# Rotary embedding in a transformer kernel: permuted operands from SBUF-to-SBUF transfers in place of permutation matmuls

## The chip, the cores and the metric

The kernel runs on one core of a Trainium2 chip. The metric is the device time of one execution in microseconds. TensorE does the matmuls, VectorE (DVE) and ScalarE (ACT) the elementwise work, GpSimd (POOL) and SyncE (SP) here issue transfers for the most part.

## The reference, cut to what matters

Three layers over 256 tokens of width 1024, batch 1, float32: an "even" mixer (stick-breaking attention and top-64 sparse attention with an index score), an "odd" mixer (differential attention), each with a gated feed-forward layer, and a third layer with a chunked recurrence over 272 positions. Queries and keys of the sparse, the index and the differential attention are turned by their position first:

```python
def apply_rope(t, cos, sin):
    t32 = t.astype(F32)
    half = t.shape[-1] // 2
    t1, t2 = t32[..., :half], t32[..., half:]
    return jnp.concatenate([t1 * cos - t2 * sin, t2 * cos + t1 * sin], axis=-1).astype(t.dtype)
...
    o_dsa = dsa_attention(apply_rope(q_dsa.reshape(b, s, N_DSA_HEADS, HEAD_DIM), cos, sin),
                          apply_rope(k_dsa[:, :, None], cos, sin)[:, :, 0],
                          v_dsa,
                          apply_rope(q_ix.reshape(b, s, N_IDX_HEADS, IDX_DIM), cos, sin),
                          apply_rope(k_ix[:, :, None], cos, sin)[:, :, 0],
                          w_ix * N_IDX_HEADS ** -0.5)
...
    q = apply_rope(q.reshape(b, s, 2 * N_DIFF_HEADS, DIFF_DIM), cos, sin).reshape(b, s, N_DIFF_HEADS, 2, DIFF_DIM)
    k = apply_rope(k.reshape(b, s, 2 * N_DIFF_HEADS, DIFF_DIM), cos, sin).reshape(b, s, N_DIFF_HEADS, 2, DIFF_DIM)
```

A head has 64 features, so a half is 32.

## The kernel before, in words

**Layout.** Features lie on partitions, tokens along the free dimension. A tile `qkv[:, n, :]` holds 128 features, two heads, of 256 tokens. The weights come as units of 128x1024 floats (512 KB), two in a 1 MB load by SyncE into `raw`. ScalarE makes `whi` of a unit (L488), VectorE the rest `wlo` (L907), and TensorE computes an output tile of a unit as 8 x 3 matmuls of 128x256 (L1764 to L1766). There are four buffers of `whi` and `wlo` (`SPLIT = 4`): the split of unit m waits until unit m - 4 is done, and both engines work three units ahead (`LEAD = 3`).

**Order.** Each engine runs its instructions in program order. The segments (even, out0, ffn0, down0, odd, out1, ...) follow each other. Within the even segment (20 units) and the odd one (24 units) the attention is written out by hand as pieces ahead of units: TensorE does `even_pieces(u)` or `diff_pieces(u)`, then unit u. VectorE does `even_first(u)` or `diff_first(u)`, then the split of unit u + 3, then `even_then(u)` or `diff_then(u)`; ScalarE likewise. In the odd segment units 0 to 2 run interleaved (`first_units`).

**Rotary embedding.** `trig` holds cosine and sine by partition and token. TensorE multiplies a tile by a constant permutation `rot`, which swaps the halves of each head and negates one, into PSUM (`rotate_even`, L1894, and `rotate`, L2119 and L2120). Keys with one head (tiles 19 and 16) are also needed on both halves of the partitions: `double_even` multiplies them by `dup` and `rotdup` (L1898, L1899). VectorE then computes tile x cos (L1132, L1368), the permuted one x sin (L1133, L1369) and their sum back into `qkv` (L1135, L1371), and counts `rope_done`. The even segment has five such steps, which this text calls rope 0 (tiles 17 and 18), rope 1 (tile 19, doubled), rope 2 (16, doubled), rope 3 (12, 13) and rope 4 (14, 15). TensorE's share stands ahead of units 4, 4, 6, 7 and 9, VectorE's in `even_first` of the same units. The odd segment has eight, rope h for tiles h and 8 + h, which are units 2h and 2h + 1: TensorE's share ahead of unit 2h + 3, VectorE's (`rope_pair`) in `diff_first(2h + 4)`.

**Who needs them.** `index_products` on TensorE ahead of unit 6 (L1913) waits for two `rope_done`; `sparse_scores`, ahead of unit 14, for five. `diff_scores(h)`, L2131, ahead of unit 2h + 6, waits for rope h and for the mask of head h - 1 (`diff_mask`, L1383, VectorE, `diff_first(2h + 5)`), whose exponentials ScalarE computes after unit 2h + 7 (L679), and whose scaling VectorE does in `diff_then(2h + 8)`.

**GpSimd.** Its queue carries the side stream: 40 loads of 1 MB of modulation weights into two buffers (`load_sides`, L2388). Load n waits until 2n - 2 side sums of VectorE are done (`side_used`). The first side sums are those after units 1, 2 and 3; the fourth is at unit 15 (`SIDE_AT`). Loads 36 to 39 wait until the odd segment's attention is done (`o_done`).

## Time and profile before

| | |
|---|---|
| median of 3 runs | 1252.2 us (1250.85 to 1258.83) |
| the profiled execution | 1251.66 us |
| its span, first to last instruction | 1249.9 us |
| mean granted TensorE clock | 0.99 |
| DMA traffic | 232.89 MB, mean 186 GB/s |
| 1 MB weight loads, median to landing | 4.9 us, 177 of them |
| 1 MB side loads, median to landing | 6.9 us, 40 of them |

The page lists busy time by engine, the span in slices, the DMA queues, the chain of work that ended last, and the costliest groups of instructions. A busy TensorE is not a TensorE at its peak, since matmuls are pipelined: their spacing says what one costs. Start times in a timeline are us from the span's start.

### The profile page before, as it was taken

To read this page: it belongs to the slowest core of one execution; us is meant where nothing else is said; L and a number is where in the kernel's file an instruction comes from. 1 tells how busy PE (TensorE), PEld (TensorE's weight loads), DVE (VectorE), ACT (ScalarE), POOL (GpSimd) and SP (SyncE) were. 2 spreads that over 40 slices of the span, in tenths; PEclk is the share of its full clock that TensorE was granted. 3 is DMA by queue.
4 is the path that set the end of the run, shared out by engine and by line. 5 is a ranking of instruction groups with operands and counts; after the bars stand their busy time and mean duration, and the time that the engine had idled before them with its cause. 6 is when DMAs were issued, how large, how long until landed. Compare 5 with 4: busy or idle time off the path is not lost.

```text
span 1249.9 us, 24570 instructions
## 1 busy us (share of the span) xinstructions
PE 1204.4 (96%) x9578; PEld 1171.2 (94%) x9578; DVE 882.8 (71%) x1448; ACT 604.8 (48%) x958; POOL 23.5 (2%) x47
## 2 busy tenths in 40 slices
PE   6999989999998999899999989999999999999997
PEld 6998889999998999899999979998999999999997
DVE  6798778888777785677664467866855685877743
ACT  1558535444344466454443456543433645555532
POOL 0000000000000000000000000000000000000000
PEclk9999989999999999999999999998989999999999
DMA  9944747978782333356455514532322363555541
GB/s 363 357 158 171 277 155 298 353 292 321 257 316 84 135 136 120 151 186 251 169 180 192 179 58 159 179 103 100 136 102 102 137 205 131 202 179 190 176 161 34
DMA packets 35364, 232.89 MB, mean 186 GB/s; under 512 B 4688, under 2 KB 7120, under 8 KB 7504
## 3 DMA queue, kind: packets, MB, share of 16 engines
q1 hardware_dynamic: 29520, 189.78, 42.4%
q0 software_dynamic: 5760, 41.95, 9.3%
q8 instruction: 58, 0.95, 0.3%
q14 instruction: 26, 0.21, 0.0%
HBM read 230.67 MB, written 1.05 MB: 185 GB/s over the span
## 4 chain that ended last, share of the span: by engine, by line
PE 85%; DVE 7%; ACT 4%; issue 3%; DMA 1%; SPq 0%; DVEq 0%; ACTq 0%
PE acc L1764 22%; PE acc L1765 21%; PE acc L1766 21%; PE aux L1764 2%; PE aux L1766 2%; PE aux L1765 2%; PE aux L2256 2%; PE aux L1871 2%; PE aux L1846 2%; ACT whi L488 1%; PE aux L1864 1%; DMA raw<-weights 1%; DVE wlo L907 1%; DVE qkv L1074 1%; PE aux L2131 0%
## 5 line engine op out<-in xcount | busy, mean ns | idle before, releaser
L1764 PE MATMUL acc<-hhi,whi 128*128 128x256 f32 (+3 forms) x1984 | 570.0, 287 | 5.5 <-DVE wlo L907 2.2
L907 DVE TENSOR_TENSOR wlo<-raw,whi 128x1024 fp32r<-128x1024 f32 x338 | 412.5, 1221 | 219.0 <-ACT whi L488 218.9
L1765 PE MATMUL acc<-hlo,whi 128*128 128x256 f32 (+3 forms) x1984 | 562.7, 284 | 0.0
L1766 PE MATMUL acc<-hhi,wlo 128*128 128x256 f32 (+3 forms) x1984 | 560.3, 282 | 0.0
L488 ACT ACTIVATE whi<-raw 128x1024 fp32r<-128x1024 f32 x338 | 356.5, 1056 | 203.1 <-PE acc L1766 186.0
L1764 PEld LDWEIGHTS acc<-hhi,whi 128*128 128x128 f32 x1984 | 376.0, 190 | 10.8 <-issue 6.8
L1766 PEld LDWEIGHTS acc<-hhi,wlo 128*128 128x128 f32 x1984 | 377.4, 190 | 0.0
L1765 PEld LDWEIGHTS acc<-hlo,whi 128*128 128x128 f32 x1984 | 376.3, 190 | 0.4
L1764 PE MATMUL aux<-ahi,whi 128*128 (+1 forms) x264 | 74.3, 281 | 0.0
L1766 PE MATMUL aux<-ahi,wlo 128*128 (+1 forms) x264 | 74.2, 281 | 0.0
L1765 PE MATMUL aux<-alo,whi 128*128 (+1 forms) x264 | 74.1, 281 | 0.0
L1764 PE MATMUL acc<-ahi,whi 128*128 (+1 forms) x264 | 74.1, 281 | 0.0
L1766 PE MATMUL acc<-ahi,wlo 128*128 (+1 forms) x264 | 74.1, 281 | 0.0
L1765 PE MATMUL acc<-alo,whi 128*128 (+1 forms) x264 | 73.9, 280 | 0.0
L1764 PE MATMUL acc<-mhi,whi 128*128 128x256 f32 (+1 forms) x192 | 56.6, 295 | 3.8 <-DVE mlo L926 3.8
L658 ACT ACTIVATE side_conv<-acc 128x256 f32<-128x256 f32 x44 | 16.9, 383 | 79.0 <-PE acc L1766 79.0
L1765 PE MATMUL acc<-mlo,whi 128*128 128x256 f32 (+1 forms) x192 | 54.7, 285 | 0.0
L1766 PE MATMUL acc<-mhi,wlo 128*128 128x256 f32 (+1 forms) x192 | 54.6, 284 | 0.0
L1765 PEld LDWEIGHTS acc<-alo,whi 128*128 128x128 f32 x264 | 49.8, 189 | 0.0
L1765 PEld LDWEIGHTS aux<-alo,whi 128*128 128x128 f32 x264 | 49.8, 189 | 0.0
L1766 PEld LDWEIGHTS aux<-ahi,wlo 128*128 128x128 f32 x264 | 49.8, 188 | 0.0
L1766 PEld LDWEIGHTS acc<-ahi,wlo 128*128 128x128 f32 x264 | 49.7, 188 | 0.0
(346 smaller groups left out, 1503.8 us busy)
## 6 DMA issues: line engine op xcount, KB each, us to landing
raw<-weights SPq DMA_DIRECT2D x177, 1024.0 KB, 4.9
lev<-side_weights POOLq DMA_DIRECT2D x40, 1024.0 KB, 6.9
x<-xT SPq DMA_DIRECT2D x1, 1024.0 KB, 8.9
out<-x SPq DMA_DIRECT2D x4, 256.0 KB, 2.2
cst<-consts SPq DMA_DIRECT2D x1, 768.0 KB, 18.2
cst<-consts SPq DMA_DIRECT2D x1, 584.0 KB, 7.8
cst<-consts SPq DMA_DIRECT2D x1, 256.0 KB, 9.5
vec<-vecs SPq DMA_DIRECT2D x1, 163.0 KB, 2.3
```

Source lines behind the costliest of these rows:

```text
L488: A(whi[:, m % SPLIT, :], raw[:, (m + MOD_UNITS) % RAW, :], ACT.Copy).then_inc(hi_ready, 1)
L658: A(side[:, k % 2, 0:t], acc[(a0 + j) % 4][:, 0:t], ACT.Silu)\
L907: v.tensor_tensor(wlo[:, m % SPLIT, :], raw[:, (m + MOD_UNITS) % RAW, :], whi[:, m % SPLIT, :].bitcast(F32), ALU.subtract).then_inc(lo_rea ...
L1074: ins = v.scalar_tensor_tensor(total, raw[:, u % RAW, :], small[:, u % KT:u % KT + 1], total, ALU.mult, ALU.add)
L1764: mm(o, whi[:, u % SPLIT, w], hi, start=start, stop=False, skip_group_check=True)
L1765: mm(o, whi[:, u % SPLIT, w], lo, start=False, stop=False, skip_group_check=True)
L1766: return mm(o, wlo[:, u % SPLIT, w], hi, start=False, stop=stop_, skip_group_check=True)
L1846: ins = mm(aux[3][:, q:q + 1], mod_sums[s_][:, P * k:P * k + P], C("ones", 1), start=True, stop=True)
L1864: ins = mm(aux[0][:, 0:t], C("mean"), view[:, n, :], start=n == 0, stop=n == KT - 1)
L1871: ins = mm(aux[1][:, 0:t], C("mean"), big[:, 0, n * t:n * t + t], start=n == 0, stop=n == KT - 1)
L2256: ins = mm(o[:, a_:a_ + 64].rearrange("p (n b) -> p n b", b=b), M_[:, h, t0:t0 + P], M_[:, h, t0:t0 + P].rearrange("p (n b) -> p n b", b=2 ...
```

## The change

The products with `rot`, `dup` and `rotdup` are removed from TensorE, with their constants. In their place GpSimd issues transfers from `qkv` to a buffer in SBUF: for a pair of tiles four of 32 partitions x 2 x 256 floats (64 KB), which swap the halves of each head; for a doubled key six, two of 64 partitions x 256 floats (64 KB) and four of 32 partitions (32 KB). There are 24 in the even segment and 32 in the odd one. The sign of the permutation goes into the sine, by a scale per partition. The buffers alternate (`side_conv` in the even segment, `big` in the odd one); VectorE waits for the transfers (`rot_loaded0`, `rot_loaded1`), and GpSimd for VectorE before a buffer is written again. The even transfers stand between side loads 2 and 3 on GpSimd's queue, the odd ones between loads 35 and 36.

```diff
@@ constants
-    ("inv", 1), ("ones", P), ("ident", P), ("rot", P), ("dup", P), ("rotdup", P), ("mean", P), ("mean_v", P),
+    ("inv", 1), ("sign", 1), ("ones", P), ("ident", P), ("mean", P), ("mean_v", P),
...
+    put("sign", np.where(i % 64 < 32, -1.0, 1.0)[:, None])
...
+EVEN_TURNED = (64, 96, 160, 160, 224)
+ODD_TURNED = (224, 160)
...
+        def even_turned(n):
+            return beside_flat[:, 512 * (n % 2):512 * (n % 2) + 512]
+
+        def odd_turned(h):
+            return big[:, 2, 512 + 512 * (h % 2):1024 + 512 * (h % 2)]
@@ ScalarE
-            A(trig[:, 1, :], tile[:, 3, 0:T1], ACT.Sin).then_inc(trig_ready, 1)
+            A(trig[:, 1, :], tile[:, 3, 0:T1], ACT.Sin, scale=C("sign", 1)).then_inc(trig_ready, 1)
@@ VectorE, even_rope
-                dve.wait_ge(rope_mm, n + 1)
+                dve.wait_ge([rot_loaded0, rot_loaded1][n % 2], EVEN_TURNED[n])
...
-                    src, rot = aux[1][:, 0:256], aux[1][:, 256:512]
+                    src, b = b[:, 0:256], b[:, 256:512]
...
-                st(v.tensor_tensor(b, rot, sin, ALU.mult))
+                st(v.tensor_tensor(b, b, sin, ALU.mult))
@@ VectorE, rope_pair
-                dve.wait_ge(rope_mm, 5 + h + 1)
+                dve.wait_ge([rot_loaded0, rot_loaded1][h % 2], ODD_TURNED[h % 2] + 64 * (h // 2 + 1))
@@ TensorE, even_pieces
-                if u == 4:
-                    rotate_even(aux[0], (17, 18), 3)
-                    double_even(19)
...
                 if u == 6:
-                    pe.wait_ge(rope_done, 2)
-                    double_even(16)
                     pe.wait_ge(vt_read, 2)
                     index_products()
-                if u == 7:
-                    pe.wait_ge(relu_done, 4)
-                    rotate_even(aux[0], (12, 13), 6)
-                if u == 9:
-                    pe.wait_ge(rope_done, 4)
-                    rotate_even(aux[0], (14, 15), 8)
@@ TensorE, diff_pieces
-                if 3 <= u <= 17 and u % 2 == 1:
-                    rotate((u - 3) // 2)
@@ GpSimd
-            load_sides(2, 36)
+
+            def turn(b, source, to, of, sem_):
+                pool.dma_start(b[to:to + 32], source[of:of + 32]).then_inc(sem_, 16)
+
+            def turn_even(n, tiles, doubled):
+
+                if n >= 2:
+                    pool.wait_ge(rope_done, n - 1)
+                sem_ = [rot_loaded0, rot_loaded1][n % 2]
+                if doubled:
+                    source, b = qkv[:, tiles, 0:T1], even_turned(n)
+                    for p0 in (0, 64):
+                        pool.dma_start(b[p0:p0 + 64, 0:256], source[0:64]).then_inc(sem_, 16)
+                        turn(b[:, 256:512], source, p0, 32, sem_)
+                        turn(b[:, 256:512], source, p0 + 32, 0, sem_)
+                else:
+                    source = qkv[:, tiles:tiles + 2, 0:T1]
+                    b = even_turned(n).rearrange("p (k t) -> p k t", k=2)
+                    for p0 in (0, 64):
+                        turn(b, source, p0, p0 + 32, sem_)
+                        turn(b, source, p0 + 32, p0, sem_)
+
+            def turn_odd(h):
+
+                for a in range(a0d + 2 * h, a0d + 2 * h + 2):
+                    acc_read(pool, None, a)
+                if h >= 2:
+                    pool.wait_ge(rope_done, 5 + h - 1)
...
+            load_sides(2, 3)
+            pool.wait_ge(even_read, 3)
+            turn_even(0, 17, False)
+            turn_even(1, 19, True)
+            pool.wait_ge(even_read, 4)
+            turn_even(2, 16, True)
+            pool.wait_ge(even_read, 6)
+            turn_even(3, 12, False)
+            pool.wait_ge(even_read, 8)
+            turn_even(4, 14, False)
+            load_sides(3, 36)
+            a0d = START["odd"][2]
+            for h in range(HEADS):
+                turn_odd(h)
```

On TensorE, at the sixth unit of the even segment: before, after unit 5 (`acc<-hhi,whi` and its kin are a unit's matmuls, L1913 the index products).

```order
165 L1766 MATMUL acc<-hhi,wlo 128x256
166 L1898 MATMUL aux<-qkv,cst 128x256 [waits rope_done]
167 L1899 MATMUL aux<-qkv,cst 128x256
168 L1913 MATMUL acc<-qkv 128x128 [waits rope_done,vt_read]
169 L1913 MATMUL acc<-qkv 128x128
170 L1913 MATMUL aux<-qkv 128x128 x2
171 L1913 MATMUL aux<-qkv 128x256 x4
172 L1764 MATMUL acc<-hhi,whi 128x256 [waits even_read,lo_ready]
```

The changed kernel at the same place (its index products are L1901):

```order
161 L1765 MATMUL acc<-hhi,wlo 128x256
162 L1901 MATMUL acc<-qkv 128x128 [waits rope_done,vt_read]
163 L1901 MATMUL acc<-qkv 128x128
164 L1901 MATMUL aux<-qkv 128x128 x2
165 L1901 MATMUL aux<-qkv 128x256 x4
166 L1763 MATMUL acc<-hhi,whi 128x256 [waits even_read,lo_ready]
```

The doubled product of tile 16 is gone, and the index products follow unit 5 directly; they still wait for two ropes.

GpSimd's queue from its first load, before:

```order
6 L2388 DMA lev<-side_weights 128x2048 [waits first_used]
7 L2388 DMA lev<-side_weights 128x2048
8 L2388 DMA lev<-side_weights 128x2048 [waits side_used] x34
9 L2388 DMA lev<-side_weights 128x2048 [waits side_used,o_done]
10 L2388 DMA lev<-side_weights 128x2048 [waits side_used] x3
```

and in the changed kernel, up to the transfers of rope 2:

```order
7 L2354 DMA lev<-side_weights 128x2048
8 L2354 DMA lev<-side_weights 128x2048 [waits side_used]
9 L2367 DMA side_conv<-qkv 32x2x256 [waits even_read]
10 L2367 DMA side_conv<-qkv 32x2x256 x3
11 L2377 DMA side_conv<-qkv 64x256
12 L2367 DMA side_conv<-qkv 32x256 x2
13 L2377 DMA side_conv<-qkv 64x256
14 L2367 DMA side_conv<-qkv 32x256 x2
15 L2377 DMA side_conv<-qkv 64x256 [waits rope_done,even_read]
16 L2367 DMA side_conv<-qkv 32x256 x2
```

The ten transfers of ropes 0 and 1 stand behind the third side load and its wait.

VectorE between its third side sum and the splits of units 7 and 8, before:

```order
56 L937 SCALAR_TENSOR_TENSOR big<-lev,small,big 128x1024 [waits side_used,side_loaded1]
57 L1132 TENSOR_TENSOR lev<-qkv,trig 128x512 [waits rope_mm]
58 L1133 TENSOR_TENSOR lev<-aux,trig 128x512
59 L1135 TENSOR_TENSOR qkv<-lev 128x2x256 [waits dve_step]
60 L1132 TENSOR_TENSOR lev<-aux,trig 128x256 [waits rope_done,rope_mm]
61 L1133 TENSOR_TENSOR lev<-aux,trig 128x256
62 L1135 TENSOR_TENSOR qkv<-lev 128x256 [waits dve_step]
63 L907 TENSOR_TENSOR wlo<-raw,whi 128x1024 [waits hi_ready,units_done] x2
```

and in the changed kernel:

```order
56 L936 SCALAR_TENSOR_TENSOR big<-lev,small,big 128x1024 [waits side_used,side_loaded1]
57 L1131 TENSOR_TENSOR lev<-qkv,trig 128x512 [waits rot_loaded0]
58 L1132 TENSOR_TENSOR side_conv<-side_conv,trig 128x512
59 L1134 TENSOR_TENSOR qkv<-lev,side_conv 128x2x256 [waits dve_step]
60 L1131 TENSOR_TENSOR lev<-side_conv,trig 128x256 [waits vt_mm,rope_done,rot_loaded1]
61 L1132 TENSOR_TENSOR side_conv<-side_conv,trig 128x256
62 L1134 TENSOR_TENSOR qkv<-lev,side_conv 128x256 [waits dve_step]
63 L906 TENSOR_TENSOR wlo<-raw,whi 128x1024 [waits hi_ready,units_done] x2
```

The instructions are as many and as large as before; they wait for transfers instead of matmuls, and the splits stand behind them as before.

## Rows read from the trace of the kernel before

**Rows 1.** The page, parts 1 and 4: engine totals, and the chain by engine.

```profile
PE 1204.4 (96%) x9578; PEld 1171.2 (94%) x9578; DVE 882.8 (71%) x1448; ACT 604.8 (48%) x958; POOL 23.5 (2%) x47
...
PE 85%; DVE 7%; ACT 4%; issue 3%; DMA 1%; SPq 0%; DVEq 0%; ACTq 0%
```

**Rows 2.** Waits of TensorE over the span: total us, times, longest.

```profile
PE aux L2119 <- DVE qkv L1371: 2.7, 1, 2.7
...
PE aux L2119 <- ACT qkv L712: 1.1, 1, 1.1
...
PE aux L2131 <- DVE small L1383: 0.6, 1, 0.6
```

**Rows 3.** Timeline of TensorE, even segment: start us, us, line, tiles, count.

```profile
48.95 0.28 PE L1766 MATMUL acc<-hhi,wlo 128*128 128x256 f32 x1
...
50.61 0.47 PE L1764 MATMUL acc<-hhi,whi 128*128 128x256 f32 x1
...
56.59 0.28 PE L1766 MATMUL acc<-hhi,wlo 128*128 128x256 f32 x1
...
57.66 0.37 PE L1913 MATMUL acc<-qkv 64*128 64x128 f32 x1
```

**Rows 4.** Timeline of VectorE, the first two ropes of the even segment.

```profile
52.33 0.68 DVE L1132 TENSOR_TENSOR lev<-qkv,trig 128x512 f32<-128x512 f32 x1
...
53.64 0.69 DVE L1135 TENSOR_TENSOR qkv<-lev 128x512 f32<-128x512 f32 x1
54.44 0.42 DVE L1132 TENSOR_TENSOR lev<-aux,trig 128x256 f32<-128x256 f32 x1
...
55.23 0.43 DVE L1135 TENSOR_TENSOR qkv<-lev 128x256 f32<-128x256 f32 x1
```

**Rows 5.** Timeline of GpSimd's queue: the third side load, and a pair.

```profile
50.37 0.53 POOL L2388 DMA_DIRECT2D lev<-side_weights  x1 [20.34 <-DVE big L937]
...
512.10 1.05 POOL L2388 DMA_DIRECT2D lev<-side_weights  x2 [153.40 <-DVE mlo L926]
```

**Rows 6.** Landing of side weights issued at 50.4, then the pair of 512.1 and 512.6.

```profile
DMA to landing us min/median/max: 7.7/7.7/7.7
...
DMA to landing us min/median/max: 7.0/9.3/11.7
```

**Rows 7.** The page, part 6: KB each, median us from issue to landing.

```profile
out<-x SPq DMA_DIRECT2D x4, 256.0 KB, 2.2
```

**Rows 8.** Busy time by stretch: us of each engine, PEclk (granted clock), DMA share, GB/s.

```profile
168.00:169.00 1.00, 0.00 (x0) 0.00 (x0) 1.00 (x2) 0.00 (x0) 0.00 (x0) 1.00 1.05 393
...
170.00:171.00 1.00, 1.00 (x3) 0.82 (x3) 1.00 (x4) 0.00 (x0) 0.07 (x1) 0.50 0.95 328
...
172.00:173.00 1.00, 1.00 (x4) 0.81 (x3) 0.39 (x1) 0.00 (x0) 0.00 (x0) 0.52 0.97 410
```

**Rows 9.** Timeline of TensorE in the odd segment.

```profile
403.37 0.28 PE L1766 MATMUL acc<-hhi,wlo 128*128 128x256 f32 x1
...
407.05 0.47 PE L1764 MATMUL acc<-hhi,whi 128*128 128x256 f32 x1
...
410.17 0.93 PE L2131 MATMUL aux<-qkv 64*128 64x128 f32 x8
...
439.03 0.28 PE L1766 MATMUL acc<-hhi,wlo 128*128 128x256 f32 x1
...
439.82 0.47 PE L1764 MATMUL acc<-hhi,whi 128*128 128x256 f32 x1
...
442.74 0.28 PE L1766 MATMUL acc<-hhi,wlo 128*128 128x256 f32 x1
...
450.83 0.93 PE L2131 MATMUL aux<-qkv 64*128 64x128 f32 x8
```

**Rows 10.** Timeline of VectorE in the odd segment: rope 0 ends, a mask ends.

```profile
405.46 0.69 DVE L1371 TENSOR_TENSOR qkv<-big 128x512 f32<-128x512 f32 x1
...
450.45 0.08 DVE L1383 DVE_READ_ACCUMULATOR2_ANT small<- 128x1 f32 x1
```

More of the change, by code:

```diff
@@ L133, in constants @@
     put("neg8", np.full((P, P), -8.0))
-    rot = np.zeros((P, P))
-    for m in range(P):
-        if m % 64 < 32:
-            rot[m + 32, m] = -1.0
-        else:
-            rot[m - 32, m] = 1.0
-    put("rot", rot)
-    dup = np.zeros((P, P))
-    dup[i % 64, i] = 1.0
-    put("dup", dup)
-    put("rotdup", rot[:, :64] @ dup[:64])
+    put("sign", np.where(i % 64 < 32, -1.0, 1.0)[:, None])
     s, q = i[:, None], np.arange(T1)[None, :]
@@ L2111, in _ @@
             a0d = START["odd"][2]
-            def rotate(h):
-                for a in range(a0d + 2 * h, a0d + 2 * h + 2):
-                    acc_read(pe, None, a)
-                if h >= 1:
-                    pe.wait_ge(rope_done, 5 + h)
-                mm(aux[0][:, 0:256], C("rot"), qkv[:, h, 0:T1], start=True, stop=True)
-                mm(aux[0][:, 256:512], C("rot"), qkv[:, 8 + h, 0:T1], start=True, stop=True).then_inc(rope_mm, 1)
             def diff_scores(h):
```

34 lines of the change are left out of this document (15 added, 19 removed).

## Prediction

> **What bounds the kernel now.** The page comes first: TensorE is busy 96% of the span and holds 85% of the chain that ended last [rows 1]. So a microsecond of TensorE work that goes is worth up to a microsecond, and one of waiting that comes costs one. The waits of TensorE say where it is not its own limit: in the odd segment it waits 2.7 us once for VectorE's rope result before L2119, 1.1 us once for ScalarE's copy, and 0.6 us once for VectorE's mask before L2131 [rows 2]. Everywhere else around the removed matmuls it runs without a gap. One unit is 24 matmuls at about 0.12 us spacing, some 2.9 us (from the end of the double product to the next piece: 407.05 to 410.17 less a little [rows 9]).
>
> **What goes from TensorE, even segment.** Before unit 4: last matmul of unit 3 at 48.95, first of unit 4 at 50.61 [rows 3], a gap of 1.66 where 0.12 is ordinary, so 1.54 us goes (four matmuls). Before unit 6: 56.59 to 57.66, 1.07 less 0.12, so 0.95 goes (two). The two pairs before units 7 and 9 are of the same kind as a pair of the odd segment, 439.03 to 439.82 [rows 9]: 0.79 less 0.12, 0.67 each, 1.3 together.
>
> **What comes in its place there.** TensorE's next need of a rope result is the index product before unit 6. It stood at 57.66 and would be reached at 57.66 - 1.54 - 0.95 = 55.2. It needs rope 0 (tiles 17, 18) and rope 1 (tile 19). Their data is fetched by ten transfers (four, then six) that stand on GpSimd's queue behind the third side load, and this was issued at 50.37, because it waits for VectorE's second side sum [rows 5]. That is after the tiles were ready, so that wait, not `even_read`, sets the start. One issue takes 0.53 us (two took 1.05 [rows 5]); no row shows one of 32 or 64 partitions, so I take the same price: 50.90 + 10 x 0.53 = 56.2 for the last. Landing: the side load itself needed 7.7 us, until 58.1 [rows 6]. Two side loads issued 0.53 us apart landed 7.0 and 11.7 us after their issues, the second some 5 us behind the first [rows 6], so the queue delivers in turn and the small transfers queue behind the megabyte. Bounds for the landing of a small one: 2.2 us (the 256 KB stores [rows 7]) and 7.7. I take 59.0 for rope 0's data and 59.8 for rope 1's, just behind the side load, since the small ones carry little. VectorE then needs 2.0 us for rope 0 (52.33 to 54.33) and 1.2 for rope 1 (54.44 to 55.66) [rows 4]: 59.0, 61.0, 62.3, and the index product starts at 62.4 instead of 57.66: **+4.7**, a stall of 7.2 us.
>
> The Trainium skill (DMA: Bandwidth & Descriptors, Anatomy of one DMA — SWDGE (gpsimd) path) fits such a transfer by 2.0 us plus its bytes at 436 GB/s, about 2.2 us for 64 KB. As an estimate by that page alone, without the queueing, rope 0's data would be there at 55.2, rope 1's at 58.4, the index product at 59.7, and the sum would come out 2.7 us lower. No run here shows it yet.
>
> **The clock.** Around 168 to 169 TensorE did nothing for some two microseconds, at a granted clock of 1.00 (2.4 GHz); at 170 it was 0.50 (1.2 GHz), and 0.52 in 172 to 173, where it rose again [rows 8]: three microseconds at half rate behind a short pause. A longer stall should do the same, **+1.5** (0 if it does not). The four removed matmuls before units 7 and 9 give **-1.3**.
>
> **VectorE behind the stall.** It is in order, and three splits of weights (`wlo`) stand behind ropes 0 to 2. Ropes 0 and 1 end with the stall, so the splits of units 7 and 8 end at 64.6, in time for units that start near 67 and 70. Rope 2's six transfers wait for rope 0 (61.0) and land near 66.5; its cover is the three units TensorE has in hand. Ropes 3 and 4 are fetched after ropes 1 and 2, while VectorE computes index scores and top rounds. VectorE is about 1.5 us later against TensorE than before, and had roughly 3 us in hand; TensorE also comes 1.3 us sooner. I put **+0.6** (0 to 3) for splits that come late. The index product, ropes 2 to 4 and GpSimd's later side loads have nobody else waiting: the fourth side load was only issued after side sums of unit 15. Even segment: 4.7 + 1.5 - 1.3 + 0.6 = **+5.5**.
>
> **Odd segment.** No side load stands between the transfers here, all of those before are out by unit 0 and the next wait for `o_done`. Each pair's four transfers may go as soon as units 2h and 2h+1 are copied, and VectorE comes to rope h some 9 us after unit 2h+1 (442.74 and the rope at about 451.6, a split behind the mask that ends at 450.53 [rows 9, 10]). Copy 0.7, issues 4 x 0.53 = 2.1, landing 2.2: 5.0. Hidden, with 4 us in hand; at a landing of 7.7 it is 10.5 and 1.5 us late. At the start, the wait before unit 5 goes: 403.37 to 407.05 [rows 9], 3.68 less 0.12, 3.56 us, and before unit 3 the 1.1 us of waiting with 0.67 of matmuls. TensorE would reach the first scores at 410.17 - 3.56 - 1.1 - 0.67 = 404.8, but rope 0 ends at 405.46 + 0.69 = 406.15 on VectorE [rows 10], which was already busy without a pause. So the scores start at 406.25 instead of 410.17: -3.9.
>
> Of the six other pairs (0.67 each) the first two should count in full: -1.3. After them a loop through the other engines decides: last matmul of a unit, ScalarE's copy, four exponentials and `whi`, then VectorE's split, scale and mask, then the scores. From 442.74 to the mask's end (450.45 + 0.08 = 450.53 [rows 10]) this is 7.79 us; the scores came at 450.83, so only 0.2 to 0.3 us is free. Without its pair TensorE arrives 0.67 earlier and waits about 0.45. The 0.6 us wait for the mask [rows 2] is this loop at the one place where no pair stands before the scores. The wait does not delay the unit that starts the next turn of the loop, so two turns together win 0.2 + 0.67, 0.44 each: four turns, -1.8. Odd segment: -3.9 - 1.3 - 1.8 = **-7.0**. Bounds: -9.1 (all of 8 x 0.67, 1.1 and 2.7), and -3.8 if the loop eats everything behind the start.
>
> The constants are 192 KB smaller and the sine takes its sign from an operand; the first is behind the weights that the first units need, the second is one instruction of the same form. Both at nothing. VectorE's ropes read SBUF instead of PSUM: the same 0.69 us for both kinds of operand in [rows 4, 10], so nothing.
>
> **Sum.** 1251.66 (profiled execution, span 1249.9 plus 1.8 around it) + 5.5 - 7.0 = 1250.2. The median before is 1252.2, within its own scatter of it. I forecast 1250.
>
> **Rivals.**
> *The even stall is small.* Issues of 32 partitions cost half (0.27), and the side load lands in 5 us: rope 0's data at 55.4, index product at 58.8, +1.1, clock 0, -1.3: -0.2. With an odd segment at -7 to -9.1: 1243 to 1244. For it: a transfer has half or less of the side load's partitions. Against it: the DMA engines are still loaded there, which is why that load took 7.7. Chance 0.17.
> *The transfers are dear and the ropes come late.* It is one mechanism, GpSimd's issue price. It turns the sign when the index product starts 1.5 us later still, at 0.53 + 0.15 = 0.68 us per issue. At 1.06 us, twice the row, the last even issue is at 61.5, landed 63.7 to 69.2, index product at 65.0 to 70.5, +7.3 to +12.8, rope 2's six issues hold split 9 (+3 in all): even +10.5 to +16; the odd transfers then need 7.1 us of 9, still hidden: -7. That gives 1255 to 1261, and at 1.5 us per issue, where the odd ropes come late too, 1265 or more. For it: the 0.53 is what the profile shows for the issuing instruction, and never more than two in a row; against it: those two were evenly spaced. Chance 0.22.
> *The loop eats the odd gain.* Odd at -3.8, even at +5.5: 1253.4. For it: at the one place without a pair nearly all of it was lost. Chance 0.14.
> *As forecast*, 1246 to 1253: 0.47.
>
> **How the numbers follow.** The forecast's own range is 1246 to 1253. The range of 8 in 10 takes in the small stall at the bottom and twice the issue price at the top: 1243 to 1261. One per cent, about what a measurement of this kernel can tell, is 12.5 us: below 1239.7 no case reaches but the sum of all lower bounds with luck, 0.04; above 1264.7 only the dear transfers with late odd ropes, 0.10; within, 0.86.
>
> **What would show it.** In the changed profile: ten issues from about 50.9 at 0.53 us spacing; VectorE idle before rope 0 until about 59; TensorE idle some 7 us before the index product, then a granted clock of 0.5 for 3 us; no wait before units 3 and 5 of the odd segment, one of 1.5 us before the first scores, and alternating waits of up to 0.5 us for the mask L1383's successor before later scores; none of VectorE for odd transfers. The forecast is wrong if an issue costs far from 0.53, if small transfers pass the side load, or if split 10 to 12 come late.

## The result

The changed kernel takes 1257.7 us (median of 20 runs, 1253.5 to 1262.6), the one before beside it 1252.4 (20 runs, 1250.3 to 1258.8): 1.0032 of the time before, 95% interval [1.0019, 1.0046]. The ratio is worked out on its own and is not the quotient of the two medians, which would be 1.0043; here and below the two differ by up to some 3 us. The forecast was 1250. The time lies within 1% of it and in the wide range (1243 to 1261), but above the range of the forecast itself (1246 to 1253), and the change cost 4 to 5 us where a gain of 2 was foreseen: the direction was wrong. Two executions that took 1674 and 2968 us, one of the kernel before and one of a kernel below, are left out of all ratios and medians.

**The profile after.** The profiled execution took 1257.8 us, its span is 1256.0 us, and its mean granted clock 0.984 (0.99 before). The page, parts 1 and 4, against [rows 1]:

```profile
PE 1197.1 (95%) x9526; PEld 1164.6 (93%) x9526; DVE 883.5 (70%) x1448; ACT 605.0 (48%) x958; POOL 53.0 (4%) x103
...
PE 80%; DVE 10%; ACT 5%; issue 3%; DMA 2%; POOL 0%; DVEq 0%; SPq 0%; ACTq 0%
```

TensorE has 52 instructions less and 7 us less to do, and the span is 6 us longer. In the chain that ended last TensorE holds 80% instead of 85%, VectorE 10% instead of 7%, and DMA 2% instead of 1%. The waits over the span (total us, times, longest), against [rows 2]:

```profile
DVE lev L1131 <- DMA side_conv<-qkv: 14.7, 2, 9.2
...
PE acc L1901 <- DVE qkv L1134: 10.0, 1, 10.0
```

Both are new and both are in the even segment: VectorE waits twice, 14.7 us in all, for transfers, and TensorE waits 10 us before the index products. The timelines of GpSimd, VectorE and TensorE there, against [rows 3 to 5]:

```profile
50.23 0.53 POOL L2354 DMA_DIRECT2D lev<-side_weights  x1 [20.25 <-DVE big L936]
50.80 2.15 POOL L2367 DMA_DIRECT2D side_conv<-qkv  x4
52.94 0.53 POOL L2377 DMA_DIRECT2D side_conv<-qkv  x1
...
54.97 0.99 POOL L2367 DMA_DIRECT2D side_conv<-qkv  x2
64.04 0.52 POOL L2377 DMA_DIRECT2D side_conv<-qkv  x1 [8.08 <-DVE qkv L1134]
```

```profile
61.43 0.69 DVE L1131 TENSOR_TENSOR lev<-qkv,trig 128x512 f32<-128x512 f32 x1 [9.16 <-DMA side_conv<-qkv]
...
64.34 0.42 DVE L1134 TENSOR_TENSOR qkv<-lev,side_conv 128x256 f32<-128x256 f32 x1
...
72.55 0.43 DVE L1131 TENSOR_TENSOR lev<-side_conv,trig 128x256 f32<-128x256 f32 x1 [5.52 <-DMA side_conv<-qkv]
```

```profile
64.91 0.55 PE L1901 MATMUL acc<-qkv 64*128 64x128 f32 x1 [10.01 <-DVE qkv L1134]
...
101.07 1.19 PE L1918 MATMUL acc<-qkv 64*128 64x128 f32 x3 [3.35 <-DVE small L1218]
```

The issues go as forecast: the side load at 50.23, then ten in a row up to 55.96 at half a microsecond each. Rope 0's data is there only at 61.4, though, and the index products start at 64.91, 7.25 us later than before (57.66). A second stall follows: rope 2's transfers are issued from 64.04 on, VectorE waits for them until 72.55, and TensorE waits 3.35 us more before the sparse scores of unit 15, which come at 101.07. These stood at 88.89 before: 12.2 us late. What the landing took (us from issue, median; issued at 50.5 to 51, then at 54.3 to 56.5, then at 64.3 to 67), against [rows 6]:

```profile
lev<-side_weights POOLq DMA_DIRECT2D x1, 1024.0 KB, 10.5
side_conv<-qkv POOLq DMA_DIRECT2D x1, 64.0 KB, 7.2
...
side_conv<-qkv POOLq DMA_DIRECT2D x3, 32.0 KB, 5.9
side_conv<-qkv POOLq DMA_DIRECT2D x1, 64.0 KB, 5.8
...
side_conv<-qkv POOLq DMA_DIRECT2D x2, 64.0 KB, 1.9
side_conv<-qkv POOLq DMA_DIRECT2D x4, 32.0 KB, 3.7
```

The side load itself took 10.5 us instead of 7.7. Beside it the ten small transfers need 5.6 to 9.0 us, and those of ropes 2 and 3 that run beside a 1 MB weight load issued at 66.07 need 4.6 to 6.0 (in the last group they are mixed with earlier ones); the first of rope 2, with nothing else in flight, need 1.7 to 1.9. They did not wait for the side load to land: it landed at 60.7, and eight of the ten had landed before, between 58.0 and 60.6. The last of rope 0 (61.4) and the last of rope 1 (62.5) came after it.

TensorE's clock, by windows (us, busy us of PE, PEld, DVE, ACT, POOL; then granted clock, DMA share, GB/s), against [rows 8]:

```profile
58.00:60.00 2.00, 0.00 (x0) 0.00 (x0) 0.00 (x0) 0.00 (x0) 0.00 (x0) 0.96 0.55 134
60.00:62.00 2.00, 0.00 (x0) 0.00 (x0) 0.57 (x1) 0.00 (x0) 0.00 (x0) 0.50 0.05 14
...
68.00:70.00 2.00, 2.00 (x10) 2.00 (x11) 0.00 (x0) 2.00 (x3) 1.14 (x3) 0.50 0.84 333
70.00:72.00 2.00, 2.00 (x18) 2.00 (x18) 0.00 (x0) 0.04 (x2) 0.00 (x0) 0.98 0.88 274
```

It was at half rate (1.2 GHz) from 60 to 70, the last 5 us of it in work. It fell again behind the 3.35 us before the sparse scores:

```profile
102.00:104.00 2.00, 2.00 (x7) 1.44 (x5) 1.26 (x6) 1.42 (x3) 0.00 (x0) 0.50 0.29 45
104.00:106.00 2.00, 2.00 (x10) 2.00 (x11) 1.96 (x4) 0.00 (x0) 0.00 (x0) 0.50 0.85 324
```

In the odd segment the scores came as forecast, against [rows 9]:

```profile
422.85 0.93 PE L2099 MATMUL aux<-qkv 64*128 64x128 f32 x8 [1.91 <-DVE qkv L1370]
...
475.58 0.93 PE L2099 MATMUL aux<-qkv 64*128 64x128 f32 x8 [0.61 <-DVE small L1382]
```

The next two fences are ScalarE's Ln of the norms behind the even segment, behind the feed-forward layer (the odd segment's start) and behind the odd layer's attention, before and after:

```profile
180.29 0.38 ACT L526 ACTIVATE std<-aux 128x256 f32<-128x256 f32 x1 [2.10 <-PE aux L1871]
...
383.81 0.38 ACT L526 ACTIVATE std<-aux 128x256 f32<-128x256 f32 x1 [2.10 <-PE aux L1871]
...
526.59 0.38 ACT L526 ACTIVATE std<-aux 128x256 f32<-128x256 f32 x1 [2.10 <-PE aux L1871]
```

```profile
196.93 0.38 ACT L525 ACTIVATE std<-aux 128x256 f32<-128x256 f32 x1 [2.09 <-PE aux L1870]
...
400.44 0.38 ACT L525 ACTIVATE std<-aux 128x256 f32<-128x256 f32 x1 [2.09 <-PE aux L1870]
...
537.20 0.39 ACT L525 ACTIVATE std<-aux 128x256 f32<-128x256 f32 x1 [2.10 <-PE aux L1870]
```

The even segment and its output are 16.6 us longer in this execution, the feed-forward layer takes the same time, and the odd stretch is 6.0 shorter (142.8 to 136.8). Of the 16.6 us, 12.2 arise up to the sparse scores. The other 4.4 arise behind them: from the scores to the norm it takes 95.9 us at a mean granted clock of 0.91, where the kernel before took 91.4 at 0.96, with the same number of matmuls. The remaining 4.5 us of the difference of the spans went the other way behind 739 us, where this execution had fewer stretches at half clock than the one before; the section on the hardware comes back to it.

### The profile page after: what moved, and what is told of

It reads as the page before. It is cut to its first block, busy times and chain, and to the rows that moved or that the text cites. A ratio compares the mean times of both kernels' runs of the same rounds, so it can differ in the third digit from the quotient of the medians.

```text
span 1256.0 us, 24523 instructions
## 1 busy us (share of the span) xinstructions
PE 1197.1 (95%) x9526; PEld 1164.6 (93%) x9526; DVE 883.5 (70%) x1448; ACT 605.0 (48%) x958; POOL 53.0 (4%) x103
## 4 chain that ended last, share of the span: by engine, by line
PE 80%; DVE 10%; ACT 5%; issue 3%; DMA 2%; POOL 0%; DVEq 0%; SPq 0%; ACTq 0%
PE acc L1763 20%; PE acc L1764 20%; PE acc L1765 20%; PE aux L1763 2%; PE aux L1765 2%; PE aux L1764 2%; DVE wlo L906 2%; PE aux L2222 2%; PE aux L1870 2%; ACT whi L487 2%; PE aux L1845 2%; PE aux L1863 1%; DVE qkv L1073 1%; DMA side_conv<-qkv 1%; DMA raw<-weights 1%
```

## The experiments

Three theories are named in the expectations. Q: the even transfers are late because of their place on GpSimd's queue, behind the third side load. C: they are late because they share the DMA engines with large loads. V: VectorE has no slack up to the sparse scores, so that each of its delays counts. Times are medians; each ratio is to the kernel before, timed beside it, with its 95% interval.

**The two halves apart.** The first takes the transfers in the odd segment only, the second in the even segment only; the other segment keeps its matmuls, with the constants it needs.

```diff
@@ odd only: TensorE, even_pieces
+                if u == 4:
+                    rotate_even(aux[0], (17, 18), 3)
+                    double_even(19)
...
@@ odd only: GpSimd
-            turn_even(0, 17, False)
...
-            turn_even(4, 14, False)
@@ even only: TensorE, diff_pieces
+                if 3 <= u <= 17 and u % 2 == 1:
+                    rotate((u - 3) // 2)
@@ even only: GpSimd
-            for h in range(HEADS):
-                turn_odd(h)
```

> The even segment keeps the matmuls with a permutation (its negative entries moved to the sine, same cost); only the odd segment fetches by transfers. Theory A (the odd segment gains what its trace shows, the loss is all in the even segment): ScalarE's first Ln of the norm after the even segment stays at 180.3 us as in the kernel before, the first scores of the odd segment come about 4 us earlier and its last ones about 7.5 us earlier than before; time about 1245 us, 6 to 7.5 us under the kernel before. Theory B (what the odd segment wins is given back later, by the granted clock or another engine): the time stays within 2 us of the kernel before, although the odd segment is shorter.

> Only the even segment fetches by transfers; the odd one keeps its matmuls. Theory A: the Ln of the norm after the even segment stands near 197 us, as in the changed kernel, 16 us later than before, and the whole is 11 to 17 us slower than the kernel before. Theory B: less than 6 us slower, since a later segment takes the loss up.

Odd only: 1245.65 us (five runs), 0.9957 of before [0.9942, 0.9973]. Even only: 1265.46 (six runs), 1.0128 [1.0100, 1.0155]. Against a median of 1252.77 beside them that is -7.1 and +12.7, together +5.6 where the whole change gave +5.3. By the ratios it is -5.4 and +16.0, together +10.6 where the whole change gave +4.0, so that the halves add up is known to some 7 us only. The traces say where each half arises: the norm behind the even segment comes at 180.5 us with odd only and at 192.4 with even only (197 was expected; 180.3 before), and the odd stretch takes 136.9 us with odd only, as in the changed kernel. So the odd term (-7.0) was right to some 2 us, and the even one (+5.5) was less than half of what it is. Odd only beats both kernels.

**What holds the first transfers up.** The third side load moves behind all even transfers; then a third buffer is added, so that rope 2's transfers follow at once instead of waiting for rope 0.

```diff
@@ GpSimd
-            load_sides(2, 3)
             pool.wait_ge(even_read, 3)
...
-            load_sides(3, 36)
+            load_sides(2, 36)
@@ and in the second kernel
-                if n >= 2:
-                    pool.wait_ge(rope_done, n - 1)
+                if n >= 3:
+                    pool.wait_ge(rope_done, n - 2)
```

> The changed kernel with the third side load moved on GpSimd's queue from ahead of the even transfers to behind them, nothing else. Theory Q (the transfers are late because they stand behind that load, in the issuing queue and in its rings): ten issues from about 47.3 us, landed by 55 us, index product at 57 to 58 us instead of 64.9, no 10 us pause of TensorE; even segment 8 to 13 us shorter than in the changed kernel. Theory C (they are late because the weights and constants in the other queue fill the DMA engines until about 58 us, whatever the order): landings still 6 to 9 us after issue, index product at 60 to 62 us, even segment only 3 to 5 us shorter.

> As the run with the third side load behind the transfers, and with a third buffer, so that the transfers of rope 2 need not wait for rope 0. Theory V (VectorE is the limit up to the first sparse scores, so each of its waits for a transfer counts): VectorE's wait before rope 2 goes, and the wait of 3.4 us of TensorE before the sparse scores of unit 15 shrinks with it; 2 to 5 us under the run before it. Rival: rope 2 is hidden by the units in hand, as the prediction had it; no difference over 1 us.

Turns first: 1252.51, 1.0007 [0.9982, 1.0032]. The issues start at 47.7, 3.1 us earlier, but the ten transfers still land after 3.5 to 6.7 us (median 5.3), and VectorE waits 3.51 for rope 0 and 5.49 for rope 2. The index products come at 59.59, between what Q (57 to 58) and C (60 to 62) had said. With three buffers: 1250.38, 0.9983 [0.9958, 1.0009]; rope 2 comes almost without a wait (0.2), rope 0 still after 4.07, and the index products at 60.25. The intervals of these two kernels overlap; the traces tell them apart. The sparse scores come at 95.70 and 92.86 instead of 101.07: of the 12.2 us that they came late, 8.2 were the place in the queue and the missing buffer. The rest is the landing: these transfers do not wait behind anything on their own queue, and still take more than twice the median of 2.3 us of the 32 transfers in the odd segment. SyncE's 1 MB weight loads and its 768 KB of masks fill the DMA engines up to 50 us, as a window of the kernel with three buffers shows (DMA share 1.03, 427 GB/s):

```profile
46.00:48.00 2.00, 2.00 (x20) 2.00 (x19) 1.95 (x3) 2.00 (x5) 0.27 (x1) 1.00 1.03 427
```

**Quiet engines.** First only the masks are loaded later, then also the 1 MB weight load that was issued at 50 us (for units 12 and 13) is held until rope 0 is done.

```diff
@@ SyncE, loads of the even segment, the second kernel (the first holds the masks only)
-            load_constants(2, masks_loaded)
...
+                    if name == "even" and j == 2:
+                        sp.wait_ge(rope_done, 1)
                     follow(None, j)
+                    if name == "even" and j == 2:
+                        load_constants(2, masks_loaded)
```

> The kernel with three buffers and the side load behind the transfers, and SyncE's 768 KB load of masks moved from 29.5 us to behind VectorE's rope 0 (about 57 us); it was among the loads that filled the DMA engines until 50 us. Theory C (the transfers are slow because they share full DMA engines): they are issued at 47.5 to 53 as before, but land after 2 to 4 us instead of 4 to 6.7; VectorE waits under 2 us for rope 0 (4.1 with the masks early), index products at 57.5 to 59 instead of 60.3, time 1247 to 1249.5. Rival (the transfers are slow by themselves, by their many short rows): landing and index products within 0.5 us of before, 1250.4.

> The kernel with the masks later, and the 1 MB weight load of 49.9 us (for units needed after 67 us) also held until VectorE's rope 0 is done. Then no load of 1 MB is issued between 45 and 56 us. Theory C (a transfer lands 2 to 3 us after its issue unless a 1 MB load runs beside it): the first three of rope 0 landed in 2.9 with the masks moved, the rest now too: rope 0's data 51 to 53 us (57.1 with the load in between), VectorE waits under 1 us for it, the last landing at 56.5, index products 57 to 58.5 (60.6 before), time 1243 to 1247. Rival (the transfers are slow by themselves, ten of them in a row): index products stay at 60 to 61, 1248.

Masks later: 1248.05, 0.9953 [0.9929, 0.9976]; the index products are still at 60.59, because the next weight load went out at 49.9 and ran beside them (VectorE was also ready for rope 0 only at 53.41, 0.8 us later than in the kernel with three buffers). The first three transfers landed in 2.3 to 3.6 us, those issued from then to 53.5 us in 3.6 to 6.9. That speaks for theory C. The engines' load while both run is a share of 0.80 at only 143 GB/s:

```profile
50.00:52.00 2.00, 2.00 (x19) 2.00 (x19) 2.00 (x2) 1.34 (x2) 2.00 (x5) 1.00 0.80 143
```

With that load held: 1248.92, 0.9955 [0.9931, 0.9980]. The landings of the transfers issued at 47.6 to 49.9 and, in the second group, of those issued at 54 to 57.5, when the two held loads had just gone out; then the index products and VectorE's rope 2:

```profile
side_conv<-qkv POOLq DMA_DIRECT2D x5, 64.0 KB, 2.2
...
raw<-weights SPq DMA_DIRECT2D x2, 1024.0 KB, 7.7
cst<-consts SPq DMA_DIRECT2D x1, 768.0 KB, 8.5
side_conv<-qkv POOLq DMA_DIRECT2D x3, 64.0 KB, 7.0
lev<-qkv POOLq DMA_DIRECT2D x3, 32.0 KB, 5.9
```

```profile
55.89 0.34 PE L1906 MATMUL acc<-qkv 64*128 64x128 f32 x1 [0.65 <-DVE qkv L1139]
```

```profile
62.28 0.43 DVE L1136 TENSOR_TENSOR lev<-lev,trig 128x256 f32<-128x256 f32 x1 [4.27 <-DMA lev<-qkv]
```

Ten transfers in a row land in 1.7 to 2.9 us when nothing large runs beside them, VectorE waits for neither rope 0 nor rope 1, and TensorE has its index products at 55.89 after 0.65 us instead of 10. So the rival of this pair (slow by themselves) falls. From 48 to 54 us, where next to nothing but these transfers moved, the share of the engines was 0.41 to 0.56 at 95 to 139 GB/s. The time did not follow (1243 to 1247 was expected): the held loads now met rope 2's transfers, which took up to 7 us, and VectorE stood still for 4.27 us there. The step missed is that a load which is held comes back; it has to miss every rope.

The Trainium skill (DMA: Bandwidth & Descriptors, Anatomy of one DMA — SWDGE (gpsimd) path) fits such a transfer by 2.0 us plus its bytes at 436 GB/s, which makes an estimate of about 2.2 us for 64 KB. The trace agrees with quiet engines (2.2) and does not beside 1 MB loads (medians of 5.9 and 7.0). The same page of the Trainium skill (Queues, rings and completion order) says, where it describes SyncE's and ScalarE's queues, that a completion is written only after every earlier write of that DMA engine, across its queues. The two groups of landings above fit that, and no run here separates it from plain sharing of the engines.

**Rope 2 kept clear too.** Masks and weight load now wait until rope 2's data has landed. Odd only ran again beside it.

```diff
-                        sp.wait_ge(rope_done, 1)
+                        sp.wait_ge(rot_loaded2, 96)
                         load_constants(2, masks_loaded)
+                    follow(None, j)
```

> The kernel with quiet engines, but the weight load of 50 us and the masks wait until rope 2's data has landed instead of until rope 0 is done, so that they no longer meet rope 2's transfers (5 to 7 us to landing there, VectorE waiting 4.3 us for them). Theories C and V together: rope 2's transfers land in 2 to 2.5 us like ropes 0 and 1, VectorE waits under 1.5 us for the masks and for nothing else, TensorE neither waits at unit 9 nor over 2.5 us before the sparse scores, and these come 31.2 to 32.5 us after the index products, as in the kernel before (31.2). All five even ropes by transfers then cost nothing, and the odd segment's gain is left: 1244 to 1247, ratio 0.993 to 0.996. Rival (something else in the even segment costs): above 1247.5.

> The odd-only kernel again, beside the kernel above on the same chip, to rank the two. It gave 1245.65, 0.9957 of before [0.9942, 0.9973]. By theories C and V the two are equal within 1.5 us, because VectorE decides when the sparse scores come in both; if TensorE's removed 3.8 us of even products counted, the kernel above would be 3 us faster.

Measured: 1249.07, 0.9964 [0.9941, 0.9986], and odd only 1242.97, 0.9917 [0.9885, 0.9948] from six runs. In the trace the first three ropes do what was expected: VectorE waits 0.87, 0 and 0 us, and rope 2's transfers land in 1.7 to 2.1. Rope 4's, issued at 63.5 beside the held loads, cost 1.98 us. The rest was missed by a little. The sparse scores come 33.3 us after the index products (31.2 to 32.5 expected), and TensorE waits 3.68 us before them (2.5 at most expected):

```profile
88.53 0.89 PE L1922 MATMUL acc<-qkv 64*128 64x128 f32 x4 [3.68 <-DVE small L1222]
```

From VectorE's readiness for rope 0 it is 37.6 us to the scores, against 36.6 in the kernel before, so 1 us is left to pay up to there. The norm comes after 127.5 us against 128.0, but with a clock of 0.98 behind the scores against 0.96. The median is 2 us above what was expected and lies where the rival had put it (above 1247.5), and the two kernels timed here side by side are 6 us apart where 1.5 was expected. Their intervals just overlap, and this kernel's overlaps more with that of the first run of odd only (0.9957). That some 1 us is left to pay in the even segment is what one trace shows; the times leave 3 to 6 us open. In this execution the stretches behind the even segment were also among those with more half clock (see the last section).

**Who sets the pace in the even segment.** Theory V says that VectorE has no slack there. The kernel before got 14 extra products on VectorE behind rope 3:

```diff
                 if u == 7:
                     even_rope(3, 12, False)
+                    dve.wait_ge(rope_done, 4)
+                    for _ in range(14):
+                        st.wait()
+                        st(v.tensor_tensor(lev[:, 0, 1088:1344], trig[:, 0, :], trig[:, 1, :], ALU.mult))
```

> The kernel before, with 14 extra products of 128x256 on VectorE behind rope 3 (their result is not used), some 0.35 to 0.4 us each, 5 to 5.6 us in all; TensorE's work is untouched. Theory V (no slack on VectorE): the sparse scores before unit 15 come later by all of it, 88.9 to about 94, and the first Ln behind the segment moves from 180.3 to 185.5 or more (more if TensorE's clock falls while it waits); time 1257.5 to 1261. Rival (the 3 us in hand of the prediction): 2 to 2.6 us later, 1254.5 to 1255.

```profile
74.38 0.39 PE L1768 MATMUL acc<-hhi,whi 128*128 128x256 f32 x1 [2.89 <-DVE wlo L907]
```

```profile
94.17 1.19 PE L1934 MATMUL acc<-qkv 64*128 64x128 f32 x3 [3.34 <-DVE small L1223]
```

1258.81, 1.0054 [1.0028, 1.0081]: 6.8 us (3.5 to 10 by the interval) for 6.4 us of work (14 x 0.46). TensorE, untouched, waits 2.89 for a split and 3.34 before the sparse scores. The 3 us in hand of the prediction are not there. The opposite edit takes five of the eight top rounds from VectorE, in the changed kernel and in the one before. Both kernels then select 24 keys instead of 64 and no longer compute the reference; they serve as probes of the time only.

```diff
-                for _ in range(TOP_AT.get(u, 0)):
+                for _ in range(TOP_AT.get(u, 0) if u >= 12 else 0):
```

> The changed kernel without the five top rounds of VectorE that stand beside units 8 to 11, so 3 of 8 rounds stay (the selection is then of 24 instead of 64 keys): 5 x 1.23 = 6.2 us of VectorE less ahead of the sparse scores before unit 15, nothing less on TensorE. Theory V (VectorE is what made the scores late there): TensorE no longer waits 3.4 us before them, nor 2 us behind; the first Ln behind the segment comes at 196.9 - 5 to 196.9 - 9, time 1248 to 1253. Rival (the stall of TensorE before the index products and the low clock behind it set the time): 1255 to 1258.

> The kernel before, without the same five top rounds (6.2 us less on VectorE). Theory V: VectorE was level with TensorE there, without slack but without delaying it, so taking work away brings at most 1 us: 1251 to 1252.5, first Ln at 179.5 to 180.5. The difference to the changed kernel without these rounds then says what the change costs where VectorE has room: the even segment's cost falls from about 12 to 3 to 6 us. Rival (VectorE already delayed TensorE before): 1246 to 1249.

The changed kernel falls from 1257.7 to 1251.57 (0.9978 of before [0.9953, 1.0002]); the one before hardly moves, 1251.61 (0.9983 [0.9958, 1.0008]). The same work taken away is worth 6 us behind the late transfers and about 1 us without them, though TensorE's stall before the index products is still there (9.48 us). TensorE no longer waits before the sparse scores:

```profile
97.78 0.92 PE L1918 MATMUL acc<-qkv 64*128 64x128 f32 x4
```

Where VectorE has room, the change as a whole costs nothing: its odd gain of 7 is met by an even cost of about 6 (3 to 6 expected). In the traces of these two the scores are 9.2 us apart (97.78 and 88.56) and the norms 6.2 (186.12 and 179.95), because the clock behind the scores was 1.00 in the one and 0.96 in the other. So part of the 6 us is the half clock that followed TensorE's wait before the scores, and went with it.

**Is it the clock?** The changed kernel with TensorE kept busy on a constant in its pause:

```diff
                 if u == 6:
+                    keep_warm(42, aux[1], C("ones"))
                     pe.wait_ge(vt_read, 2)
                     index_products()
```

> The changed kernel with 42 matmuls of 128x128 on a constant (about 0.22 us each, result not used) on TensorE in the 10 us in which it waits for ropes 0 and 1, so that it never stands still there. The granted clock should stay at 1.00 from 55 to 75, where it was 0.5 for ten us. Theory V (VectorE decides when the sparse scores before unit 15 come): units 6 to 14 come up to 5 us earlier, but the scores stay at 101 within 0.6 and TensorE waits 3 to 5 us longer before them; time as the changed kernel, 1256 to 1259. Rival (the low clock is a cost of its own): scores and everything behind them 2 to 5 us earlier, 1253 to 1255.5.

```profile
60.00:62.00 2.00, 2.00 (x20) 2.00 (x20) 1.81 (x3) 0.00 (x0) 0.00 (x0) 1.00 0.00 0
...
66.00:68.00 2.00, 2.00 (x18) 1.67 (x16) 0.00 (x0) 1.74 (x5) 1.88 (x4) 1.00 0.65 229
```

The clock stays at 1.00 (2.4 GHz) through the pause and behind it up to 80 us, and the time is 1259.89, 1.0054 [1.0032, 1.0077], no better than the changed kernel. Units 6 to 8 ran at full rate and TensorE then waited, 2.03 us for a split at 80.2 and 1.83 before the scores at 99.95 (3 to 5 were expected before the scores alone). The scores are only 1.1 us earlier than in the changed kernel, and VectorE had its data for rope 0 after 7.36 us instead of 9.16. So the half clock from 60 to 70 did not set when the scores come; VectorE's lateness did. Behind the scores the picture is less clear: this profiled execution took 1252.19 us, the fastest of eleven, and reached the norm 5.5 us before the changed kernel's (191.43), 91.5 us after the scores at a clock of 0.96 instead of 95.9 at 0.91. Whether the median holds a part of that the runs don't show.

**Two more ropes in the even segment.** Odd only, with ropes 3 and 4 by transfers as well, for which the prediction counted -1.3; it was timed twice.

```diff
@@ odd only, TensorE
-                if u == 7:
-                    pe.wait_ge(relu_done, 4)
-                    rotate_even(aux[0], (12, 13), 6)
-                if u == 9:
-                    pe.wait_ge(rope_done, 4)
-                    rotate_even(aux[0], (14, 15), 8)
```

> The kernel with only the odd segment changed, and in the even segment ropes 3 and 4 (before units 7 and 9) by transfers as well; ropes 0 to 2 stay matmuls. TensorE loses two pairs of products, 2 x 0.67 = 1.3 us of work. Theory V (up to the sparse scores before unit 15 VectorE is the limit, it has no idle time between 61.5 and the scores): the scores stay at 88.9 within 0.4 us, TensorE waits 1.3 us longer before them, the first Ln behind the segment stays at 180.5 within 0.6, and the time stays at that of the odd-only kernel (1245.7; ratio to before 0.995). Rival (TensorE is the limit, as the prediction counted these pairs): all of that 1.3 us earlier, 1244.3.

> The same kernel as with two ropes of the even segment and the odd segment by transfers, a second time, since its 0.9921 of before [0.9893, 0.9948] came from six runs and its trace shows no gain in the even segment over the odd-only kernel (0.9957). Theory V: 0.995 to 0.996 again, 1245 to 1247. Rival (the two pairs do bring something): 0.992 to 0.994, 1242 to 1244.5.

1242.04 from six runs (0.9921 [0.9893, 0.9948]) and 1247.52 from twelve (0.9953 [0.9924, 0.9982]); odd only gave 1245.65 and 1242.97. No difference between the two kernels shows. TensorE reaches the sparse scores earlier and waits for VectorE there, 2.0 and 1.8 us, where it waited for nothing with the matmuls in place.

**One table for all of them.** `start` is when VectorE was ready for rope 0, `wait` what it then waited for its data, `idle` its idle time from there to the sparse scores before unit 15, `scores` when TensorE starts these, and `work` = scores - start - wait - idle (us, from each profiled execution). The two kernels with fewer top rounds have less work on VectorE and are left out, and the second executions of odd only and of two more ropes too.

```
                          start   wait   idle   scores   work
before                    52.33   0      2.47    88.89   34.1
after                     52.27   9.16   5.52   101.07   34.1
odd only                  52.38   0      2.47    88.96   34.1
even only                 50.94   8.64   5.58    99.27   34.1
turns first               52.61   3.51   5.49    95.70   34.1
three buffers             52.61   4.07   2.16    92.86   34.0
masks later               53.41   3.71   1.31    92.53   34.1
quiet engines             52.42   0      4.27    90.79   34.1
rope 2 kept clear         50.89   0.87   2.55    88.53   34.2
two more ropes            51.00   0      2.45    87.81   34.4
VectorE busier            51.16   0      2.46    94.17   40.6
kept busy                 52.79   7.36   5.65    99.95   34.2
```

In eleven of twelve kernels the sparse scores come 34.0 to 34.4 us of VectorE's work after rope 0 could start, plus whatever VectorE stood still; in the twelfth it had 6.4 us more to do. TensorE's own work in the stretch, with or without its matmuls of the ropes, does not show: VectorE was level with it or behind it in each of the twelve. The 2.47 us of idle in the kernel before is a wait for ScalarE's `whi` of unit 9: it is what a late rope 2 could use up for nothing, and the only slack. For the changed kernel 9.16 + 5.52 - 2.47 = 12.2 us, just what the scores came late.

## Why the prediction was wrong

- **Issues: right.** From 50.80 (50.90 said), 0.5 us each (0.53) for ten in a row, so the rival of a dear issue fell as a mechanism. That its range of times (1255 to 1261) holds the result is luck.
- **Landing of ropes 0 and 1: mis-sized, and not by the mechanism given.** "59.0 for rope 0's data" was 61.4. The prediction had the small ones queue behind the side load and come just after it. The side load took 10.5 us instead of the 7.7 of [rows 6], and eight of the ten landed before it; with no side load in front (turns first) they still took 3.5 to 6.7 us, and with nothing large beside them 1.7 to 2.9. They were slow because they ran beside large loads, not because they stood behind one. That rope 0 came near to the side load's landing (60.7) was chance. The index products started at 64.91 (62.4 said), +7.25 for +4.7.
- **Clock: there, but not what sets the scores.** Half rate for 5 us of work (3 said); keeping it up brought the scores 1.1 us and the median nothing. The prediction had no term for the half clock behind TensorE's wait before the sparse scores; in the profiled execution the stretch behind them took 4.4 us more.
- **VectorE behind the stall: the step that failed.** "Had roughly 3 us in hand", +0.6, was argued from how far splits run ahead of TensorE. The trace of before had the answer. These are VectorE's last gap ahead of the sparse scores, its reading of the result that they wait for, and the scores:

```profile
61.52 1.23 DVE L907 TENSOR_TENSOR wlo<-raw,whi 128x1024 fp32r<-128x1024 f32 x1 [2.47 <-ACT whi L488]
```

```profile
88.66 0.08 DVE L1219 DVE_READ_ACCUMULATOR2_ANT small<- 128x1 f32 x1
```

```profile
88.55 0.28 PE L1766 MATMUL acc<-hhi,wlo 128*128 128x256 f32 x1
88.89 0.89 PE L1930 MATMUL acc<-qkv 64*128 64x128 f32 x4
```

  From 61.52 on VectorE has no gap, it is ready at 88.74, and TensorE, done with its unit at about the same time, takes the scores 0.15 us later. VectorE's chain (rope 0 to the top rounds to the scores) was as long as TensorE's, and the waits of [rows 2] don't show a chain that is level. So each microsecond VectorE waits counts in full, and each that TensorE saves there counts nothing: by the table -1.54, -0.95 and -1.3 were no gains. The stretch must be read as 9.16 + 5.52 - 2.47 = +12.2, and even only measured +12.7. Against the +5.5 of the forecast that is 6.7 us more: 2.6 in the landing (7.25 for 4.7), and 4.1 in the terms behind it, which were +0.8 in all (+1.5 - 1.3 + 0.6) where the sparse scores fell back by another 4.9 us.
- **Rope 2: missed in its price.** "Its cover is the three units TensorE has in hand" covered TensorE's weights and not VectorE, which stood still for 5.5 us of it. Its six transfers were issued from 64.04 on (61.0 said), met a 1 MB weight load, and the last was there at 72.5 (66.5 said).
- **Odd segment: right.** First scores: 422.85 is 12.7 us later than 410.17, against 16.6 us of shift at both ends of the layer before, so 3.95 us won (3.9 said), with a wait of 1.91 for VectorE in front (1.5 said). Waits of 0.6 us before every second score, 7.5 us won by the last (466.45 to 475.58), and 1.5 given back in the output behind: -6.0 in the profiled execution, -7.1 and -9.1 by the two medians of odd only (-7.0 said). The transfers landed in 2.3 us in the median (2.2 said), those of ropes 1 and 2, issued beside a 1 MB weight load, in 4.3 and 5.7; that was inside the 4 us in hand, and VectorE waited for none.
- **Small slips in the working.** The rival of a small stall gives 1242.4 to 1244.5 by its own terms, not 1243 to 1244. The "same 0.69 us for both kinds of operand" is not in [rows 4, 10]: the 512-element rows there have no operand in PSUM, and the 256-element ones have 0.42 against 0.43. VectorE's total (883.5 us against 882.8) bears the reading out.

In one line: forecast +5.5 - 7.0, measured +12.7 - 7.1 (medians of the two halves).

## What to carry to other kernels

Before work moves from the engine that is busy 96% to a queue, read the timeline of the engine that will wait for that queue: if it has no gap between that point and the next place where the two meet, its waits count in full and the work taken from the busy engine may count for nothing, whatever the table of waits says. Price small transfers by what else is in flight at their time, not by their size, and keep them where no megabyte is being loaded; here the same kind of transfer gave -7 us in the odd segment, where it had time to land, and +13 in the even one, where it met large loads and an engine without slack. Of such a change keep the half that pays: transfers in the odd segment only give 0.9957 and 0.9917 of the time before.

## What the runs showed of the hardware

- A transfer of 32 to 64 KB from SBUF to SBUF, issued by GpSimd, lands in 1.7 to 2.9 us with quiet DMA engines (quiet engines, 47 to 53 us). Beside 1 MB loads it takes longer: 3.5 to 6.7 beside SyncE's weights (turns first), 5.6 to 9.0 with a side load of GpSimd's own queue in flight too (the changed kernel). GpSimd spends 0.50 to 0.56 us per issue, also for ten in a row.
- A small transfer does not wait for a 1 MB load issued before it on the same queue: eight of ten landed before the side load did.
- Small transfers keep the DMA engines busy out of proportion: alone they took a share of 0.41 to 0.56 at 95 to 139 GB/s (quiet engines, 48 to 54 us), where large loads moved 427 GB/s at 1.03. An estimate from these numbers is 1.7 to 1.8 times the share for each byte.
- TensorE's granted clock fell to 0.50 behind pauses of 1.3 to 10 us, but not behind each: after the same wait of 1.47 us for VectorE it fell at 848 us in the kernel before (up to 860) and stayed at 1.00 in the changed one, at 858. The next such wait brought it down in both (906 to 914, 912 to 920).
- From the even segment's norm to the last Ln, the profiled executions with the odd change took 1052.2 to 1052.4 us in seven cases and 1055.9 to 1063.1 in the other five; odd only gave 1052.4 the first time and 1063.1 the second. Four of the five long ones have stretches at half clock between 840 and 880, of the short ones none. So one and the same kernel can differ by some 10 us behind the even segment. The medians of one kernel timed twice differ by 2.7 us (odd only) and 5.5 us (two more ropes); that these half-clock stretches are the reason is likely but not shown, and what decides which of them an execution gets stays open. From the sparse scores to the norm it is the same: 88.3 us at a mean clock of 1.00 (masks later), 91.4 at 0.96 (before), 95.9 at 0.91 (after).
